# Norm weights folded into the rotation tables, the queries' root folded into the exponential, and the gated norm's scaling issued inside the attention stream

## What is computed

```python
def qk_heads(p, g, rope):                       # p: (1, n, 512), 8 groups of 64
    t = rms_norm_2(p.reshape(b, n, 4, 2, 64), g)   # x * rsqrt(mean(x*x) + 1e-6) * g
    return t if rope is None else axial_rope(t, *rope)

def axial_rope(t, cos, sin):                    # t as (..., axis 2, half 2, 16)
    t1, t2 = t[..., 0, :], t[..., 1, :]
    return stack([t1 * cos - t2 * sin, t2 * cos + t1 * sin], axis=-2)

def diff_attn(q, k, v, lam):                    # latent queries see 512 keys
    s = einsum("bqhmd,bkhmd->bhmqk", q, k) * (64 ** -0.5)
    p = softmax(s, axis=-1)
    return einsum("bhqk,bkhd->bqhd", p[:, :, 0] - lam * p[:, :, 1], v)

def chunk_gmlp(pa, P):                          # the gated branch "a"
    u, v = split(gelu(pa), 2)
    v = layer_norm(v, P["ln_v_g"], P["ln_v_b"])
    gate = einsum("hpq,bnqhd->bnphd", P["w_s"], vb) + b_s
    return u * gate

def conformer_conv(pc, P):                      # the convolution branch "c"
    a, g = split(pc, 2)
    y = dwconv(a * sigmoid(g), P["conv_w"], P["conv_b"])      # 31 taps
    return silu(layer_norm(y, P["ln_c_g"], P["ln_c_b"]))

# yb = rms_norm_2(o, subln_g) * (1 - lam_init);  out = concat([ya, yb, yc]) @ w_out
```

## Time and profile before

| what | value |
|---|---|
| median of three runs | 2361.36 us (2355.01 to 2364.14) |
| profiled execution, whole | 2365.68 us |
| its span, first to last instruction | 2364.0 us |
| TensorE / VectorE / ScalarE / GpSimd busy | 94% / 59% / 45% / 13% |
| mean granted TensorE clock | 0.968 |
| TensorE busy from 1998 to 2014 us (projections, layer 1) | 11.98 of 16 us |
| TensorE busy from 1436 to 1452 us (start of attention, layer 0) | 4.89 of 16 us |
| TensorE busy from 1460 to 1526 us (attention, layer 0) | 46.39 of 66 us |

### The profile page before, as it was taken

How to read it: one execution, slowest core, us unless ns; L and a number is a source line. 1 busy time by engine, 2 the same in 40 slices (tenths; PEclk the granted TensorE clock), 3 DMA queues, 4 the chain that set the end, 5 groups by cost and what they waited for, 6 DMA issues and landing times. The chain is left out here.

```text
span 2364.0 us, 31904 instructions
## 1 busy us (share of the span) xinstructions
PE 2223.3 (94%) x12288; PEld 1810.5 (77%) x12288; DVE 1391.2 (59%) x2199; ACT 1059.5 (45%) x1767; POOL 302.2 (13%) x322
## 2 busy tenths in 40 slices
PE   8999999999999999989999997699999998889988
PEld 6777777778877777767788885588888887669987
DVE  4655476544456554765455589755555236876764
ACT  4545455444444454554445555533232225654442
POOL 0004422000000036221000134100000001500000
PEclk9998899999999998999999998799999999999999
DMA  7655333466656553344666441223333333434554
GB/s 227 200 171 169 108 121 116 162 222 205 223 195 206 179 191 114 107 138 152 231 177 196 135 132 45 72 73 116 107 107 100 114 89 99 142 116 152 179 180 140
DMA packets 171845, 349.32 MB, mean 148 GB/s; under 512 B 11824, under 2 KB 23216, under 8 KB 171696
## 3 DMA queue, kind: packets, MB, share of 16 engines
q1 hardware_dynamic: 171696, 347.29, 45.1%
HBM read 346.19 MB, written 1.05 MB: 147 GB/s over the span
## 5 line engine op out<-in xcount | busy, mean ns | idle before, releaser
L921 DVE TENSOR_TENSOR wlo<-wraw,whi 128x1024 fp32r<-128x1024 f32 (+1 forms) x535 | 646.5, 1221 | 647.1 <-ACT whi L1124 644.6
L1124 ACT ACTIVATE whi<-wraw 128x1024 fp32r<-128x1024 f32 (+1 forms) x552 | 558.5, 1027 | 564.8 <-PE psum L1915 246.4
L1915 PE MATMUL psum<-whi,act_h 128*128 128x512 f32 (+2 forms) x1424 | 574.4, 403 | 20.3 <-DVE modT L1507 6.8
L1915 PE MATMUL psum<-wlo,act_h 128*128 128x512 f32 (+2 forms) x1424 | 554.3, 389 | 0.0
L1915 PE MATMUL psum<-whi,act_l 128*128 128x512 f32 (+2 forms) x1424 | 554.2, 389 | 0.0
L1915 PEld LDWEIGHTS psum<-whi,act_h 128*128 128x128 f32 x1424 | 272.4, 191 | 87.8 <-issue 22.0
L1915 PEld LDWEIGHTS psum<-whi,act_l 128*128 128x128 f32 x1424 | 272.0, 191 | 56.9
L1915 PEld LDWEIGHTS psum<-wlo,act_h 128*128 128x128 f32 x1424 | 273.0, 192 | 48.3
L1915 PE MATMUL psum<-act_h,whi 128*128 128x256 f32 (+1 forms) x736 | 247.6, 336 | 11.2 <-DVE ft L1490 3.3
L1915 PE MATMUL psum<-act_l,whi 128*128 128x256 f32 (+1 forms) x736 | 243.1, 330 | 0.0
L1915 PE MATMUL psum<-act_h,wlo 128*128 128x256 f32 (+1 forms) x736 | 242.8, 330 | 0.0
(11 more groups left out here) (275 smaller groups left out, 2692.7 us busy)
## 6 DMA issues: line engine op xcount, KB each, us to landing
wraw<-in_w_in SPq DMA_DIRECT2D x136, 512.0 KB, 4.4
wraw<-in_w_gate SPq DMA_DIRECT2D x104, 512.0 KB, 4.2
wraw<-in_w_mod_pieces SPq DMA_DIRECT2D x96, 512.0 KB, 4.8
wraw<-in_w_ffn_in SPq DMA_DIRECT2D x80, 512.0 KB, 4.4
wraw<-in_w_ffn_out SPq DMA_DIRECT2D x44, 512.0 KB, 4.3
wraw<-in_w_down SPq DMA_DIRECT2D x44, 512.0 KB, 3.9
wraw<-in_w_val SPq DMA_DIRECT2D x40, 512.0 KB, 3.9
wraw<-in_w_branch SPq DMA_DIRECT2D x32, 512.0 KB, 5.0
```

Source lines behind the costliest of these rows:

```text
L921: eng.tensor_tensor(wlo[:, i, 0:st.n, 0:st.w], wraw[:, st.s % RING_W, 0:st.n, 0:st.w], whi[:, i, 0:st.n, 0:st.w].bitcast(F32), ALU.subtrac ...
L1124: nc.scalar.activation(whi[:, d % RING_S, 0:st.n, 0:st.w], wraw[:, s % RING_W, 0:st.n, 0:st.w], ACT.Copy).then_inc(sem("slab_rounded"), 1)
L1915: return nc.tensor.matmul(out, lhsT, rhs, start=start, stop=stop)
```

## The change

Four things are done differently, in the second block only.

1. A table `turn2` is built once a layer, in `qk_sums` of the keys: the norm weight of each column times cosine and times sine, for queries and keys and both latent tiles (eight VectorE instructions of 64 elements a row). `qk_scale` of a latent tile then multiplies the raw columns by both tables in two instructions of 512 elements and combines them in two of 256.
2. The queries are no longer scaled by their root. GpSimd computes the root with 1/8 in it (`rsqrt(sum + 64 eps)`), the maximum of the raw scores is multiplied by it (`tensor_tensor` for `tensor_scalar`), and the exponential takes it as a scale for each row. Two waits (`rooted`) stand before these. Keys keep the instruction that scales them.
3. `qk_scale` waits for the one before it by semaphore (`qk_normed`), and for queries it waits for the squares, not for the root.
4. `aln[1]` leaves the projections and goes into the attention's stream at turn 3; `agate` moves from turn 2 to 4, `cback` with `ln` from 4 to 5, `ln_scale` with `csilu` from 6 to 7.

```diff
@@ in plan_second
-        others += [(16, gelu), (18, aln[0]), (19, aln[1])]
+        others += [(16, gelu), (18, aln[0])]
...
+                st.rooted = [("qk_rstd", q_roots + t + 1)]
...
-            if i == 2:
+            if i == 3:
+                stream.append(aln[1])
+            if i == 4:
                 agate = Step(kind="agate", l=l, tiles=T, n=aln[0].n, banks=[pl.gemm_bank(), pl.gemm_bank()])
                 stream.append(agate)
-            if i == 4:
+            if i == 5:
                 cback = Step(kind="cback", l=l, tiles=T, banks=[pl.gemm_bank() for i in range(T // 2)])
                 cln = ln(C_C, 2, drained(*cback.banks))
                 stream += [cback, cln[0]]
-            if i == 6:
+            if i == 7:
                 stream += [cln[1], Step(kind="csilu", l=l, tiles=T, n=cln[0].n)]
@@ GpSimd, qk_sums
-                        rstds(v, v, B_QK, "qk_rstd")
+                        if st.i:
+                            rstds(v, v, B_QK, "qk_rstd")
+                        else:
+                            rstds(v, v, 1, "qk_rstd", B_QK * EPS)
@@ ScalarE, att2_e
                     act.wait_ge(sem("att2_max"), st.q + 1)
+                    need(act, st.rooted)
...
-                                             scale=B_QK ** -0.5, bias=nm2[:, st.q % 4, m:m + 1],
+                                             scale=ssq[:, st.t * 16 + 2 * st.h + m:st.t * 16 + 2 * st.h + m + 1], bias=nm2[:, st.q % 4, m:m + 1],
@@ VectorE, qk_sums of the keys
+                        for i, t, j in ((i, t, j) for i in range(2) for t in range(2) for j in range(2)):
+                            o, g = (a.rearrange("p (a i d) -> p a i d", a=2, i=2) for a in (turn2[:, i, t, j], qkg[:, i, :]))
+                            step(dve.tensor_tensor(o, g, cossin2[:, t, j].unsqueeze(2).to_broadcast([P, 2, 2, 16]), ALU.mult))
@@ VectorE, qk_scale
-                    dve.wait_ge(sem("qk_rstd"), st.sq0 + st.t + 1)
...
-                    step(dve.tensor_tensor(v, v, ssq[:, t * 16 + i * 8:t * 16 + i * 8 + 8].unsqueeze(2).to_broadcast(
-                        [P, 8, B_QK]), ALU.mult))
-                    settle()
-                    ins = dve.tensor_tensor(v, v, qkg[:, i, :].unsqueeze(1).to_broadcast([P, 8, B_QK]), ALU.mult)
+                    need(dve, [("qk_normed", st.sq0 + t)])
+                    if i:
+                        dve.wait_ge(sem("qk_rstd"), st.sq0 + t + 1)
+                        step(dve.tensor_tensor(v, v, ssq[:, t * 16 + i * 8:t * 16 + i * 8 + 8].unsqueeze(2).to_broadcast(
+                            [P, 8, B_QK]), ALU.mult))
+                    else:
+                        dve.wait_ge(sem("qk_sq"), st.sq0 + t + 1)
+                    settle()
                     if t < 2:
...
+                        r = [spin[:, j * 512:(j + 1) * 512] for j in range(2)]
+                        for j in range(2):
+                            step(dve.tensor_tensor(r[j].rearrange("p (g d) -> p g d", d=B_QK), v,
+                                                   turn2[:, i, t, j].unsqueeze(1).to_broadcast([P, 8, B_QK]), ALU.mult))
                         settle()
-                        step(dve.tensor_tensor(r[0], lo, c, ALU.mult))
-                        step(dve.tensor_tensor(r[1], up, s, ALU.mult))
-                        step(dve.tensor_tensor(r[2], lo, s, ALU.mult))
-                        settle()
-                        step(dve.tensor_tensor(lo, r[0], r[1], ALU.subtract))
-                        settle()
-                        step(dve.tensor_tensor(r[0], up, c, ALU.mult))
-                        settle()
-                        ins = dve.tensor_tensor(up, r[0], r[2], ALU.add)
+                        v, c, s = (a.rearrange("p (g i d) -> p g i d", g=16, i=2) for a in [half] + r)
+                        step(dve.tensor_tensor(v[:, :, 0, :], c[:, :, 0, :], s[:, :, 1, :], ALU.subtract))
+                        ins = dve.tensor_tensor(v[:, :, 1, :], c[:, :, 1, :], s[:, :, 0, :], ALU.add)
+                    else:
+                        ins = dve.tensor_tensor(v, v, qkg[:, i, :].unsqueeze(1).to_broadcast([P, 8, B_QK]), ALU.mult)
                     ins.then_inc(sem("qk_normed"), 1)
@@ VectorE, att2_s
-                    dve.tensor_scalar(nm, nm, B_QK ** -0.5, None, ALU.mult).then_inc(sem("att2_max"), 1)
+                    need(dve, st.rooted)
+                    g = st.t * 16 + 2 * st.h
+                    dve.tensor_tensor(nm, nm, ssq[:, g:g + 2], ALU.mult).then_inc(sem("att2_max"), 1)
```

More of the change, by code:

```diff
@@ L77, in __init__ @@
         self.ssq0, self.t, self.k0, self.sq, self.n0, self.pool, self.split, self.d = ssq0, t, k0, sq, n0, pool, split, d
-        self.parts, self.rest, self.rounds = parts, rest, []
+        self.parts, self.rest, self.rounds, self.rooted = parts, rest, [], ()
         self.after = list(after)
@@ L521, in plan_second @@
             more = dict(l=l, i=i, tiles=tiles, waits=landed(g), sq0=pl.now("qk_sq"))
+            if i == 0:
+                q_roots = pl.now("qk_sq")
             pl.tick("qk_sq", tiles)
@@ L874, in build @@
         spin = aT[:].rearrange("p i n -> p (i n)")
+        turn2 = sb("turn2", [P, 2, 2, 2, B_QK], F32, two)
         lnsq = sb("lnsq", [P, 4, A_W], mybir.dt.bfloat16, two)
@@ L1028, in done, with rstds @@
                 pool.wait_ge(sem("pool_step"), steps)
-            def rstds(out, ssq, width, ready):
-                done(pool.tensor_scalar(out, ssq, 1.0 / width, EPS, ALU.mult, ALU.add))
+            def rstds(out, ssq, width, ready, eps=EPS):
+                done(pool.tensor_scalar(out, ssq, 1.0 / width, eps, ALU.mult, ALU.add))
                 pool.tensor_tensor(out, out, minus_half[:, 0:out.shape[1]], ALU.pow).then_inc(sem(ready), 1)
@@ L1579, in _ @@
                     settle()
-                    ins = dve.tensor_tensor(v, v, qkg[:, i, :].unsqueeze(1).to_broadcast([P, 8, B_QK]), ALU.mult)
                     if t < 2:
-                        step(ins)
-                        v = half.rearrange("p (g a i d) -> p g a i d", g=8, a=2, i=2)
-                        lo, up = v[:, :, :, 0, :], v[:, :, :, 1, :]
-                        c, s = (cossin2[:, t, j].unsqueeze(1).to_broadcast([P, 8, 2, 16]) for j in range(2))
-                        r = [spin[:, j * 256:(j + 1) * 256].rearrange("p (g a d) -> p g a d", g=8, a=2) for j in range(3)]
-                        settle()
-                        step(dve.tensor_tensor(r[0], lo, c, ALU.mult))
-                        step(dve.tensor_tensor(r[1], up, s, ALU.mult))
-                        step(dve.tensor_tensor(r[2], lo, s, ALU.mult))
-                        settle()
-                        step(dve.tensor_tensor(lo, r[0], r[1], ALU.subtract))
-                        settle()
-                        step(dve.tensor_tensor(r[0], up, c, ALU.mult))
-                        settle()
-                        ins = dve.tensor_tensor(up, r[0], r[2], ALU.add)
+                        r = [spin[:, j * 512:(j + 1) * 512] for j in range(2)]
```

## The result

The changed kernel takes 2349.36 us (median of 14 runs, 2344.55 to 2355.57) against 2362.51 us of the kernel before on the same chip (14 runs, 2354.97 to 2367.61): ratio 0.9949, 95% interval 0.9938 to 0.9961, so 12 to 13 us, or 0.5%, faster. The forecast was 2347.5 us. The profiled execution has a span of 2350.6 us.

The account below looks back on a forecast made before the run. VectorE bounds layer 1's projections, TensorE layer 0's; layer 0's attention is a ring with no engine full. 6.0 + 1.0 + 4.9 + 0 + 2.0 + 0 = 13.9 us off 2365.7, less 4.3 for the median: 2347.5 us, range 2339 to 2357.

Parts of the forecast that it names:

- Layer 1's rotation and scaling: Layer 1's projections: shorter `qk_scale` on key and query tiles takes 6.0 us off VectorE's string, all on the path.
- Tables: Layer 1's projections: eight short table instructions fit where VectorE idles for the squares; cost 0, bound +1.0 us.
- Clock in layer 1: Layer 1's transposes: a shorter wait before them may keep the clock up; at most 2.5 us, taken as 1.
- Layer 0's attention, start: Before layer 0's first exponential: the gated norm's scaling leaves the front; 4.9 of its 6.8 us count.
- `ln_scale` in the stream: Layer 0's attention: its 2.85 us fit into VectorE's 3.79 us wait for GpSimd's root; cost 0, bounds -0.9 and +4.
- `csilu` behind the last exponential in layer 0: End of layer 0's attention: second table load goes and unit 15 isn't held; 2.0 us gained, bounds 0 and 3.9.
- Layer 1's attention: Layer 1: earlier start against `csilu` possibly holding the last product with v; taken as 0, bounds -1.5 and +2.
- New forms: Exponential's scale from SBUF and `nm` product taken as free; upper bound 3.6 us of ScalarE, a third in the ring.
- The product on `nm` held: Layer 0's attention: GpSimd's adds could hold some 4 of 16 products, 1.06 us each, adding 4 us: 2358.
- the stream takes its scaling back: Rival, attention: GpSimd's adds hold `ln_scale` (+4) and `csilu` saves nothing in layer 0; about 2354 us, chance 0.25.
- The one that goes slower by the clock: Rival, layer 0's attention: sparser TensorE runs at the lower clock; 10 to 30 us more (2357 to 2377), chance 0.05.

Follow-up runs that it names:

- x8: The changed kernel run again with nothing edited; ratio 0.9948 (0.9930 to 0.9965) to the kernel before.
- x1: The changed kernel with its stream put back, so tables and queries' root alone; ratio 0.9971 (0.9960 to 0.9981) to the kernel before.
- x10: The kernel before with only the gated branch's `ln_scale` moved into the stream at turn 2, right before `agate`; ratio 0.9998 (0.9984 to 1.0012).
- x4: The changed kernel with `cback` back at turn 4 and `csilu` at 6 in layer 1 only; ratio 0.9938 (0.9920 to 0.9957) to the kernel before.
- x2: The kernel before with the four moved stream steps alone; ratio 0.9958 (0.9943 to 0.9973).
- x11: The kernel before with only `ln_scale` and `csilu` of the convolution branch moved from turn 6 to 7; ratio 1.0000 (0.9982 to 1.0018).
- x5: The kernel before with the exponential reading its factor 1/8 from an SBUF column instead of an immediate; ratio 0.9993 (0.9977 to 1.0009).
- x9: The kernel before with `cback` and `ln` moved from turn 4 to 5, `ln_scale` and `csilu` from 6 to 7; ratio 1.0023 (1.0003 to 1.0042).

## Why the prediction was right

The total was right to 2 us, and the two large terms, 6.0 and 4.9, were right as sizes and as mechanisms. Several small ones were wrong in both directions. That the sum came out so near is in part luck: over the stages that the change touches (L0, P, Q, R) after has gained 10.6 us and x8 10.9, where 13.9 were forecast. Without the low stretch of 1.6 us that the profile of before has in R these are 9.0 and 9.3. The other 2 to 4 us of the 13 between the medians have no term in the sum.

- **Layer 1's rotation and scaling, 6.0.** P is 5.8 us shorter, in every profile that has the edit. 2.73 and 1.99 us a tile were forecast as 2.73 and 2.01. The added wait between the context key tiles costs 0.3, not 0.1. The wait before the transposes was forecast at 2.2 and is 1.95.
- **Tables, 0.** Right: 1.16 us, and the sum of squares behind them still waits 0.19 us for ScalarE, so they were wholly covered.
- **Clock in layer 1, 1.0.** Q fell by 0.9 in x1; after took 2.4 and x8 1.7, of which `ln_scale` in front is 1.5 (x10: 44.5 to 43.0), so 0.2 to 0.9. But it isn't the wait's length that decides: x1, after, x4 and x8 waited 1.97, 1.95, 1.97 and 1.97 us; the transposes of x4 and x8 took 4.5 us, those of the other two 3.1, though x8 and after are the same program.
- **Layer 0's attention, start, 4.9.** Right: A -4.9 in every run with that edit.
- **`ln_scale` in the stream, 0.** As it is placed, nearly: B 36.1 for 36.2 in x2, with 0.8 us of clock to its favour (units 0 to 3 take 9.1 us for 9.9, at a mean clock of 0.81 for 0.66). It was held there (2.63 us for 1.66), yet fits into the wait of 3.79 us, which is gone. But this term stands on `agate` being a turn later, which the prediction let pass as issuing the same instructions: x10 shows 6.4 us in B without it.
- **`csilu` behind the last exponential in layer 0, 2.0.** In x2: D -5.2, E +2.3, C +1.1: 1.8. On the kernel before, alone, it gives 0 (x11). The size was right for a mechanism half seen: the gain before unit 15 was larger than the 3.9 us that I took as bound, and the tail behind it takes 2.3 back. The forecast for the three terms of layer 0 was 6.9; x2 has 6.8.
- **Layer 1's attention, 0 (-1.5 to +2).** Front -1.5; R +1.8 and +2.5, and since before had a low stretch of 1.6 us in R that these have not, +3.4 and +4.1 without that stretch: 1.9 to 2.6 us lost, at the bound's end and beyond. The wait was named in the prediction (`csilu` holds the last product with v) and is there, 2.38 us; its size was taken as 0 against the earlier start.
- **New forms, 0.** Wrong, the term mis-sized. The exponential is 0.09 us longer each time (682 to 771 ns), which costs 1.4 us in layer 0 in the old order (x5) and 0.9 in the new (x8 against x2), and 0.2 to 0.3 in layer 1. That is 1.2 us in all, the bound of a third of 3.6 us. The row that I had in hand, a copy with and without a scale from SBUF (76 ns), was near it in size. (The Trainium skill, "ScalarE: Activation LUTs", section "What ACT_TABLE_LOAD costs", says that each operand read from a column adds about 93 ns to such an instruction; the measured 89 ns agree, and by it the term would have been an estimated 4.5 us of ScalarE, a third of it 1.5.)
- **The product on `nm` held.** The rival that priced it (four times in layer 0, 1.06 us each) had the number and the size right: 1.24, 1.20, 1.18, 0.66 us. But it is no cost of the new form, as x2 shows, and the 4 us that the rival made of it did not come: x2 has the holds too, and its L0 is 6.8 us shorter than before, with 6.9 forecast without them.

The rival "the stream takes its scaling back" was the right worry at the wrong turn: it is what x10 does. The one that goes slower by the clock didn't come: 0.83 for 0.82 in layer 0's attention.

What stays open: the single terms inside layer 0 are good to some 1.6 us only, since low stretches of the clock move between executions; why `cback`'s later place costs 2.6 us alone and saves 1.8 with the rest moved was read from ScalarE's order in part, not tried by itself; and of R's +6.4 in x9 against +3.8 in x11, 1.2 us are the step from unit 2 to unit 3 (6.4 us for 5.2, at a clock of 0.69 for 0.86), and the rest wasn't followed.

## What to carry to other kernels

Moves in an interleaved order are not additive: in layer 0 moves that gain 6.8 us together lost 3.5, 2.6 and nothing when one or two were made alone, and the same step one turn later lost 2.6 us in one order and won 1.8 in another. So price an order as a whole, and for each moved step look at what stands right behind it on every engine that it visits. Fold a scale into a later instruction only where the engine that is relieved is the bound; in layer 0 the scaling was free and the fold cost 0.9 us. Before explaining 1 to 2 us between two profiles, take a second profile of the same program, and look where the difference lies and what the clock was there: a growth of 1.7 us that looked like the exponential's was 1.4 us of clock.

## What the runs showed of the hardware

- An exponential with bias and scale both from SBUF takes 0.77 us for 512 elements, with an immediate scale 0.68; for 256 elements 0.55 and 0.46.
- TensorE's granted clock after a wait of 2.6 us fell to its lower level or stayed, in executions of one and the same program; such a stretch costs 1.6 us where TensorE bounds.
- VectorE instructions of 2 or 4 elements a row took 1.2 us in place of 0.17 beside GpSimd's adds, with one SBUF tensor (`tensor_scalar`) as with two; each ended 0.01 to 0.03 us behind the end of such an add.
